# Sparse and differential attention step: the first attention takes its sample tile second and tile 7 last

## The chip, the cores and the metric

The kernel runs on one core of one Trainium2 chip. The metric is the device time of one execution in microseconds, as the median of several runs. Engines are called by the names of the profile: PE is TensorE (PEld its weight loads), DVE VectorE, ACT ScalarE, POOL GpSimd, SP SyncE, which issues the DMAs.

## The reference, cut to what matters

The program is one inference step of two layers over 1024 prompt tokens and 32 sample tokens, with model width 1024. Layer 0 has a sparse attention ("A"), layer 1 a differential one ("B"); each is followed by an output product with layer norm, and by a feed-forward part. The change lies in attention A:

```
dots = einsum('bthd,bsd->bths', qi, ki)              # indexer: 8 heads
score = einsum('bths,bth->bts', relu(dots), wi * IDX_SCALE)
_, sel = top_k(score, n_sel)                         # 256 of the prompt's keys, 40 of the sample's 160
logits = einsum('btcgd,btkcd->btcgk', q, k_sel) * 64 ** -0.5
logits = logits - slopes * abs(q_pos - sel)          # ALiBi; keys beyond the chunk limit at -inf
out = einsum('btcgk,btkcd->btcgd', softmax(logits), v_sel)
```

The prompt attends to itself in chunks of 64 tokens; the 32 sample tokens attend to 128 cached keys and their own 32. The kernel doesn't gather keys: it makes a mask for each query from the scores, adds it to the distances, and runs the attention over all keys of the tile.

## The kernel before

**Tiles and steps.** `mixer_a` cuts the queries into nine tiles: tile t of 0 to 7 has 128 queries and 128(t+1) keys, and the sample tile (number 8, `SAMPLE`) has 32 queries and 160 keys. For each tile 16 heads are worked off in 8 steps of two heads; `g` counts these steps, 0 to 71, and `heads(g)` gives tile, key group and head of a step. There are 72 steps and three more for the pipeline to drain.

**What a step does.** All engines run through the same `g`, each with its own list of work:

- PE in step g: turn the probabilities of step g-2 (`turn_over`, L634), compute the logits of step g (L619, for which the reads of step g-1 must be over), in steps 0 to 5 one or two thirds of the last projection pieces (`beside`, L588), multiply the turned probabilities of step g-2 with the values (`multiply`, L653), and on even steps turn the outputs of two finished steps (L662).
- DVE in step g: on even steps scale outputs (L998, L1000); copy every second group of turned probabilities of step g-2 out of PSUM (L991; L987 and L988 for the sample); read both heads' logits of step g (L977), adding the mask and taking the extreme of each row. Behind that come two mask operations (`islice(later, 2)`).
- ACT in step g: the other half of the copies (L754; L750 and L751 for the sample), the exponentials (L741), and the outputs' copy (L763).

**Masks.** Tiles 0 and 1 need no selection, their masks are set up in front. For tiles 2 to 7 a bit search in front of the loop finds each query's threshold. Then `masking(t)` turns scores into the mask in place, on DVE: subtraction of the threshold (L922), count (L926), tie mark (L930) and a small one (L931), scan over the ties (L936), three products (L940, L945, L950), in seven yields. `settle()` (L895 to L911, four yields, two of them counts at L902) adjusts the thresholds of tiles 6 and 7. `mask_sample()` finds the sample's 40 keys by five rounds of maximum and replace (L960, L962) and makes the mask (L966, L969), six yields. They all share `tie`, `rank` and small columns, and wait for each other through `s_mask`.

**Order around the change.** The tiles run in the order 0 to 7, then the sample. In tile t, DVE makes the mask of tile t+2: two yields behind each step's reads until that generator is empty, what is left of it at the start of the next tile at the latest. So masking is in the first four steps of tiles 0 to 5 and the sample's in the first three of tile 6; settling comes right behind tile 4's mask, in tile 2.

**Around the loop.** POOL has split the projection weights into high and low parts (L122, L124); its last pair of these, for the output product, starts when the last projection piece is done. After step 74 all of PE, ACT and DVE pass a barrier (`phase_over`). Behind it `out_norm` splits outputs and far weights (L1699, L1744, L1710, L1762, and POOL at L1617 and L1620), and PE multiplies (L1685).

Of the kernel before, what the change touches and what calls it, by code (L numbers as in the profile page):

```python
# [21 lines left out]
QT = SEQ // P  # L22
SAMPLE = QT
# [362 lines left out]
def mixer_a(c):  # L386
# [59 lines left out]
    ON_ACT = (6, 7)  # L446
    ON_DVE = (2, 3, 4, 5)
    NA, ND = len(ON_ACT), len(ON_DVE)
    ranked = list(range(2, QT))
    slope = lambda c2, m, h: 2.0 ** (-(4 * (2 * c2 + m) + h + 1) / 2)  # L450
    STEPS = 9 * 8

    def score(t):
# [6 lines left out]
    def height(t):  # L460
        return P if t < QT else NEW
# [21 lines left out]

    def heads(g):

        t, p = divmod(g, 8)
        c2, j, i = p // 4, p // 2 % 2, p % 2
        return t, c2, j, i

    def groups(t):  # L490
        b = first_blocks(t)
        return [b[j:j + 4] for j in range(0, len(b), 4)]

    def turns(g):

        gs = groups(g // 8)
        return [(m, j) for m in (0, 1) for j in range(len(gs))]

    turns_before, act_before, dve_before = [0], [0], [0]
    for g in range(STEPS):  # L500
        n = len(turns(g))
# [60 lines left out]
    def tensor(pe):  # L562
# [60 lines left out]
                        mm.then_inc(s_logit, 1)  # L623

        def turn_over(g, k):
            t, n = g // 8, height(g // 8)
            m, j = turns(g)[k]
            seq = turns_before[g] + k
            pe.wait_ge(s_exp, 2 * g + m + 1)
            if seq >= 2:  # L630
                pe.wait_ge(s_pv, seq - 1)
            for x, blk in enumerate(groups(t)[j]):
                key, size = P * (4 * j + x), NEW if blk == VNEW else P
                mm = nc.tensor.transpose(bank(c, 4 + k % 2)[0:size, P * x:P * x + n], prob[0:n, g % 3, m, key:key + size],  # L634
                                         c.ident[0:n, 0:n])
            mm.then_inc(s_tr, 1)
# [18 lines left out]
            mm.then_inc(s_pv, 1)  # L655

        def turn_outputs(grp):
            t = grp // 4
            n = height(t)
            pe.wait_ge(s_norm, grp + 1)  # L660
            for m in (0, 1):
                mm = nc.tensor.transpose(bank(c, 6 + grp % 2)[:, P * m:P * m + n],  # L662
                                         o_nat[0:n, grp % 2, m].rearrange("p i d -> p (i d)"), c.ident[0:n, 0:n])
            mm.then_inc(s_ot, 1)
# [9 lines left out]
        pe.wait_ge(s_ones, 1)  # L674
        for g in range(STEPS + 3):
            n = len(turns(g - 2)) if 2 <= g < STEPS + 2 else 0
            for k in range(min(2, n)):
# [14 lines left out]
    def scalar(act):  # L692
# [42 lines left out]
                rows(*ROWS_AFTER[sub])  # L735

        def exps(g, m):
            t = g // 8
            L, n, sl = keys_of(t), height(t), g % 3
            act.wait_ge(s_read, 2 * g + m + 1)  # L740
            nc.scalar.activation(prob[0:n, sl, m, 0:L], prob[0:n, sl, m, 0:L], ACT.Exp,  # L741
                                 bias=lowest[0:n, 2 * sl + m:2 * sl + m + 1], scale=-1.0).then_inc(s_exp, 1)

        def copy_turned(g, k):
            t = g // 8
            m, j = turns(g)[k]
            act.wait_ge(s_tr, turns_before[g] + k + 1)
            b = bank(c, 4 + k % 2).rearrange("p (x q) -> p x q", x=4)
            if t == SAMPLE:
                nc.scalar.activation(pt[:, k, 0, 0:NEW], b[:, 0, 0:NEW], ACT.Copy)  # L750
                nc.scalar.activation(pt[0:NEW, k, 1, 0:NEW], b[0:NEW, 1, 0:NEW], ACT.Copy).then_inc(s_cpa, 1)  # L751
            else:
                e = len(groups(t)[j])
                nc.scalar.activation(pt[:, k, 0:e, :], b[:, 0:e], ACT.Copy).then_inc(s_cpa, 1)  # L754

        def take_output(grp):
            t = grp // 4
            c2, j = grp // 2 % 2, grp % 2
            n = height(t)
            act.wait_ge(s_ot, grp + 1)  # L760
            src = bank(c, 6 + grp % 2, 2 * P).rearrange("p (m q) -> p m q", m=2)[:, :, 0:n]
            dst = c.o_col[:, 4 * c2:4 * c2 + 4, P * t:P * t + n].rearrange("p (m j) q -> p m j q", j=2)[:, :, j]
            nc.scalar.activation(dst, src, ACT.Copy).then_inc(s_oe, 1)  # L763

        for x, (t, ch, part) in enumerate(cells):
            n, size = height(t), cell_keys(x)[0]
# [15 lines left out]
        for b in range(31):  # L782
# [6 lines left out]
            for sub in in_pass(b):  # L789
                after(sub)  # L790
        for g in range(STEPS + 3):
            n = len(turns(g - 2)) if 2 <= g < STEPS + 2 else 0
# [13 lines left out]
    def vector(v):  # L806
# [7 lines left out]
        for x, (t, ch, part) in enumerate(cells):  # L814
            n, L, size = height(t), keys_of(t), cell_keys(x)[0]
# [34 lines left out]
        for t in ranked:  # L850
            L, j = keys_of(t), slice(t - 2, t - 1)
# [127 lines left out]
                                           lowest[0:n, 2 * sl + m:2 * sl + m + 1]).then_inc(s_read, 1)  # L979

        def copy_turned(g, k):
            t = g // 8
            m, j = turns(g)[k]
            v.wait_ge(s_tr, turns_before[g] + k + 1)
            b = bank(c, 4 + k % 2).rearrange("p (x q) -> p x q", x=4)
            if t == SAMPLE:
                nc.vector.tensor_copy(pt[:, k, 0, 0:NEW], b[:, 0, 0:NEW])  # L987
                nc.vector.tensor_copy(pt[0:NEW, k, 1, 0:NEW], b[0:NEW, 1, 0:NEW]).then_inc(s_cpv, 1)  # L988
            else:
                e = len(groups(t)[j])  # L990
                nc.vector.tensor_copy(pt[:, k, 0:e, :], b[:, 0:e]).then_inc(s_cpv, 1)  # L991

        def scale_outputs(grp):
            n = height(grp // 4)
            v.wait_ge(s_pv, turns_before[2 * grp + 2])
            o = bank(c, 6 + grp % 2, 260)[0:n].rearrange("p (x d) -> p x d", x=4)
            inv = inverse[0:n, 4 * (grp % 2):4 * (grp % 2) + 4].rearrange("p (x a) -> p x a", a=1)
            nc.vector.reciprocal(inv, o[:, :, 64:65]).then_inc(s_inv, 1)  # L998
            v.wait_ge(s_inv, grp + 1)
            nc.vector.tensor_tensor(o_nat[0:n, grp % 2].rearrange("p m i d -> p (m i) d"), o[:, :, 0:64],  # L1000
                                    inv.to_broadcast([n, 4, 64]), ALU.mult).then_inc(s_norm, 1)

        later = ()
        for g in range(STEPS + 3):
            if g % 8 == 0 and g < STEPS:
                t = g // 8
                for _ in later:
                    pass
                if t + 2 <= SAMPLE:
                    later = itertools.chain(masking(t + 2) if t + 2 < QT else mask_sample(), settle() if t == 2 else ())  # L1010
                if t >= 2:
                    v.wait_ge(s_mask, masks)
            n = len(turns(g - 2)) if 2 <= g < STEPS + 2 else 0
            if g >= 4 and g % 2 == 0:
                scale_outputs((g - 4) // 2)
            if n:
                copy_turned(g - 2, 1)
            if g < STEPS:
                read_logits(g, 0)
            if n > 2:  # L1020
                copy_turned(g - 2, 3)
            if g < STEPS:
                read_logits(g, 1)
                for _ in itertools.islice(later, 2):
                    pass
# [1536 lines left out]
```

## Time and profile before

| what | value |
|---|---|
| median of 3 runs | 3197.73 us (3195.79 to 3198.46) |
| profiled execution | 3199.4 us, of which its span is 3197.5 us |
| mean granted clock of TensorE | 0.982 |
| TensorE busy | 3074.4 us, 96% |
| VectorE busy | 1513.2 us, 47% |
| ScalarE busy | 884.6 us, 28% |
| GpSimd busy | 1015.5 us, 32% |
| attention A's loop, first reads to barrier | 281.7 to 623.7 us |

The profiled execution is one run; its span reaches from its first to its last instruction, and 1.9 us of its time lie around the span. It stands 1.7 us above the median. The loop that the change touches is 342 of these 3197 us. A granted clock of 1.00 is 2.4 GHz for TensorE and 0.50 is 1.2 GHz; a value between them is a stretch with some of both. Matmuls overlap, so a group of them shows a busy time from the first start to the last modelled end.

### The profile page before, as it was taken

How to read it: one execution, taken by the hardware profiler on the slowest of the kernel's cores; microseconds unless marked ns; L12 is line 12 of the kernel's file. 1: busy time of each engine (PE TensorE's matmuls, PEld its weight loads, DVE VectorE, ACT ScalarE, POOL GpSimd, SP SyncE). 2: the span in 40 equal slices, each digit the busy share in tenths (PEclk: the TensorE clock that was granted, in tenths of full speed). 3: DMA queues.
4: the chain of work that ended last, by engine and by line, in shares of the span. 5: the costliest groups of instructions: out<-in, count | busy, mean ns of one | idle time of the engine just before them, and what ended most of it. 6: DMA issues, size and time to landing. Idle time of an engine off the chain costs nothing.

```text
span 3197.5 us, 49157 instructions
## 1 busy us (share of the span) xinstructions
PE 3074.4 (96%) x19621; PEld 2880.4 (90%) x19621; DVE 1513.2 (47%) x2914; ACT 884.6 (28%) x1915; POOL 1015.5 (32%) x495
## 2 busy tenths in 40 slices
PE   8799999899999999999989999989999999999996
PEld 8498777688999999999988999977899999999996
DVE  1898855543533343333454555565345333343335
ACT  2476544342111101111134544453300111100112
POOL 2132000135543333433242222214444433333422
PEclk9899999899999999999999999999999999999998
DMA  2122000112311111111012111111222111111101
GB/s 87 28 61 53 1 1 1 41 40 73 95 53 46 46 46 39 52 46 46 14 57 63 43 49 50 37 41 66 70 85 60 52 46 46 46 46 39 52 0 55
DMA packets 209372, 149.75 MB, mean 47 GB/s; under 512 B 28914, under 2 KB 195764, under 8 KB 209236
## 3 DMA queue, kind: packets, MB, share of 16 engines
q1 hardware_dynamic: 209236, 147.85, 15.5%
q8 instruction: 96, 1.57, 0.2%
q14 instruction: 40, 0.33, 0.0%
HBM read 128.09 MB, written 19.73 MB: 46 GB/s over the span
## 4 chain that ended last, share of the span: by engine, by line
PE 88%; DVE 6%; ACT 2%; issue 2%; POOL 1%; DMA 1%; SPq 0%; POOLq 0%; ACTq 0%; DVEq 0%
PE psum L153 49%; PE psum L2081 16%; PE psum L1685 6%; PE psum L653 4%; DVE junk L867 2%; PE psum L634 2%; PE psum L619 2%; PE psum L1273 2%; PE psum L1247 2%; PE psum L1261 1%; PE psum L588 1%; PE psum L572 1%; DVE bias L826 1%; PE psum L1222 0%; PE psum L1639 0%
## 5 line engine op out<-in xcount | busy, mean ns | idle before, releaser
L153 PE MATMUL psum<-x_hi,w_hi 128*128 128x352 f32 (+1 forms) x3192 | 1040.9, 326 | 10.0 <-POOL x_lo L1628 4.1
L153 PE MATMUL psum<-x_hi,w_lo 128*128 128x352 f32 (+1 forms) x3192 | 1027.7, 322 | 0.0
L153 PE MATMUL psum<-x_lo,w_hi 128*128 128x352 f32 (+1 forms) x3192 | 1027.6, 322 | 0.0
L122 POOL TENSOR_TENSOR w_hi<-w_raw,zeros 128x1024 fp32r<-128x1024 f32 (+1 forms) x209 | 381.5, 1825 | 1522.6 <-PE psum L153 939.2
L153 PEld LDWEIGHTS psum<-x_hi,w_hi 128*128 128x128 f32 (+1 forms) x3192 | 601.6, 188 | 12.1 <-issue 11.3
L153 PEld LDWEIGHTS psum<-x_lo,w_hi 128*128 128x128 f32 (+1 forms) x3192 | 602.4, 189 | 0.5
L153 PEld LDWEIGHTS psum<-x_hi,w_lo 128*128 128x128 f32 (+1 forms) x3192 | 601.0, 188 | 0.4
L124 POOL TENSOR_TENSOR w_lo<-w_raw,w_hi 128x1024 fp32r<-128x1024 f32 (+1 forms) x209 | 485.8, 2324 | 16.4
L2342 DVE TENSOR_TENSOR gate<-psum,gate 128x352 f32<-128x352 f32 x120 | 63.0, 525 | 725.3 <-PE psum L153 725.3
L2081 PE MATMUL psum<-h_hi,w_hi 128*128 128x352 f32 x1056 | 341.2, 323 | 1.2 <-DVE h_lo L2364 1.0
L2081 PE MATMUL psum<-h_lo,w_hi 128*128 128x352 f32 x1056 | 338.6, 321 | 0.0
L2081 PE MATMUL psum<-h_hi,w_lo 128*128 128x352 f32 x1056 | 338.4, 320 | 0.0
L2307 DVE TENSOR_TENSOR o_col<-psum,o_col 128x352 f32<-128x352 f32 x528 | 263.3, 520 | 157.4 <-PE psum L2081 155.2
L2081 PEld LDWEIGHTS psum<-h_hi,w_hi 128*128 128x128 f32 x1056 | 198.3, 188 | 1.9 <-issue 1.6
L2081 PEld LDWEIGHTS psum<-h_lo,w_hi 128*128 128x128 f32 x1056 | 198.6, 188 | 0.0
L2081 PEld LDWEIGHTS psum<-h_hi,w_lo 128*128 128x128 f32 x1056 | 198.1, 188 | 0.0
L2346 DVE TENSOR_TENSOR h_lo<-gate,h_hi 128x352 fp32r<-128x352 f32 x120 | 198.0, 1675 | 0.0
L653 PEld LDWEIGHTS psum<-valsA,ptA 128*128 128x128 f32 (+1 forms) x1216 | 145.1, 188 | 38.3 <-issue 17.5
L2236 ACT ACTIVATE h_hi<-gate 128x352 fp32r<-128x352 f32 x120 | 59.8, 498 | 426.9 <-DVE gate L2342 426.9
L653 PE MATMUL psum<-valsA,ptA 128*128 128x65 f32 (+1 forms) x1216 | 162.7, 277 | 3.9 <-DVE ptA L991 3.0
L2233 ACT ACT_TABLE_LOAD x20 | 25.7, 1283 | 478.8 <-PE psum L153 460.0
L1458 DVE CUSTOM_DVE_ANT_0 probB<-psum,distB 128x128 f32<-128x128 f32 (+5 forms) x144 | 96.4, 707 | 123.3 <-PE psum L1247 122.4
(461 smaller groups left out, 4085.3 us busy)
## 6 DMA issues: line engine op xcount, KB each, us to landing
w_raw<-in_ffn_w_dram SPq DMA_DIRECT2D x132, 512.0 KB
w_raw<-in_b_w_in_dram SPq DMA_DIRECT2D x24, 512.0 KB
w_raw<-in_ple_w_gate_dram SPq DMA_DIRECT2D x16, 512.0 KB
x_nat<-in_x_prompt_dram SPq DMA_DIRECT2D x8, 512.0 KB, 8.2
w_raw<-in_a_w_in_dram SPq DMA_DIRECT2D x8, 512.0 KB
w_raw<-in_a_w_in_dram SPq DMA_DIRECT2D x16, 256.0 KB
x_rows<-x_rows SPq DMA_DIRECT2D x8, 512.0 KB, 2.6
out_new_b_v_prompt_dram<-valsB SPq DMA_DIRECT2D x8, 512.0 KB, 3.3
```

The source lines that it names most:

```text
L122: nc.gpsimd.tensor_tensor(c.w_hi[s][:, 0:kc], c.w_raw[s][:, 0:kc], zero, ALU.add).then_inc(c.split[s], 1)
L124: nc.gpsimd.tensor_tensor(c.w_lo[s][:, 0:kc], c.w_raw[s][:, 0:kc], c.w_hi[s][:, 0:kc].bitcast(F32), ALU.subtract).then_inc(c.split[s], 1)
L153: last = c.nc.tensor.matmul(out, w, x, start=(n == 0), stop=(n == 3 * len(terms) - 1))
L619: mm = nc.tensor.matmul(c.psum[0:n, 1024 * m + a:1024 * m + a + size], queries[rows, 4 * c2 + 2 * i + j, q:q + n], keys[rows, c2, key:key ...
L634: mm = nc.tensor.transpose(bank(c, 4 + k % 2)[0:size, P * x:P * x + n], prob[0:n, g % 3, m, key:key + size], c.ident[0:n, 0:n])
L653: mm = nc.tensor.matmul(c.psum[0:n, at:at + 65], pt[0:size, k, x, 0:n], vals[0:size, blk, 2 * c2 + m, :], start=(j == 0 and x == 0), stop= ...
L867: nc.vector.tensor_scalar(junk[t][:, :], score(t), level[:, t - 2:t - 1], 0.0, ALU.is_ge, ALU.add, accum_out=count[:, t - 2:t - 1]).then_i ...
L1458: nc.vector.tensor_tensor_reduce(prob[:, sl, m, 0:L], c.psum[:, 1024 * m:1024 * m + L], dist[:, o:o + L], slope(h), -LOWEST, ALU.add, ALU.min,
L1685: mm = nc.tensor.matmul(out, o[t % 2][:, u, 0:n], ww[:, cols], start=(j == 0 and x == 0), stop=(j == KC - 1 and x == 2))
L2081: mm = nc.tensor.matmul(o, w[s][:, m, :], h[:, j, piece(t)], start=(j == 0 and k == 0), stop=(j == 1 and k == 2))
L2307: nc.vector.tensor_tensor(o, src, o, ALU.add).then_inc(s_da, 1)
L2346: nc.vector.tensor_tensor(h_lo[:, j, piece(done)], gate[:, 1, piece(done)], h_hi[:, j, piece(done)].bitcast(F32), ALU.subtract).then_inc(s ...
```

## The change

The tiles run in the order 0, sample, 1, 2, ... 7. All functions that derived the tile from `g` or from the group of outputs now look it up in `TILES`. The masks are made in that same order by one generator, `all_masks()`: sample, 2, 3, 4, 5, settling, 6, 7. It runs on without regard to tile boundaries, two yields a step, until it is empty; at the start of a tile only what that tile still lacks is made first. What each mask computes is unchanged.

```
+    TILES = (0, SAMPLE, 1, 2, 3, 4, 5, 6, 7)
...
     def heads(g):
-        t, p = divmod(g, 8)
-        c2, j, i = p // 4, p // 2 % 2, p % 2
-        return t, c2, j, i
+        p = g % 8
+        return TILES[g // 8], p // 4, p // 2 % 2, p % 2
...
     def turns(g):
-        gs = groups(g // 8)
+        gs = groups(TILES[g // 8])
...
-            t, n = g // 8, height(g // 8)
+            t = TILES[g // 8]
+            n = height(t)
...
-            t = grp // 4
+            t = TILES[grp // 4]
...
-        later = ()
+        made = {0, 1}
+
+        def all_masks():
+            settled = False
+            for t in TILES:
+                if t < 2:
+                    continue
+                if t in ON_ACT and not settled:
+                    settled = True
+                    yield from settle()
+                yield from mask_sample() if t == SAMPLE else masking(t)
+                made.add(t)
+
+        later = all_masks()
         for g in range(STEPS + 3):
             if g % 8 == 0 and g < STEPS:
-                t = g // 8
-                for _ in later:
-                    pass
-                if t + 2 <= SAMPLE:
-                    later = itertools.chain(masking(t + 2) if t + 2 < QT else mask_sample(), settle() if t == 2 else ())
+                t = TILES[g // 8]
+                while t not in made:
+                    next(later, None)
                 if t >= 2:
                     v.wait_ge(s_mask, masks)
```

The lines that change a tile's lookup in `exps`, `copy_turned` (ACT and DVE), `take_output` and `scale_outputs` are of the same kind and are left out here.

## Rows read from the trace of the kernel before

**Rows 1.** The page: one engine line of busy times, and the chain by engine.
```profile
PE 3074.4 (96%) x19621; PEld 2880.4 (90%) x19621; DVE 1513.2 (47%) x2914; ACT 884.6 (28%) x1915; POOL 1015.5 (32%) x495
...
PE 88%; DVE 6%; ACT 2%; issue 2%; POOL 1%; DMA 1%; SPq 0%; POOLq 0%; ACTq 0%; DVEq 0%
```

**Rows 2.** Windows: tile 1, tile 3, sample's first part and rest.
```profile
core 0: us, PE busy (x) PEld busy (x) DVE busy (x) ACT busy (x) POOL busy (x), PEclk, DMA share, GB/s
...
303.25:322.34 19.09, 17.84 (x127) 12.84 (x128) 15.54 (x57) 11.07 (x28) 0.00 (x0) 1.00 0.09 29
...
347.98:379.41 31.43, 30.99 (x226) 23.61 (x226) 24.07 (x57) 16.81 (x28) 0.00 (x0) 1.00 0.01 1
...
604.55:610.40 5.85, 5.85 (x71) 4.15 (x72) 3.55 (x22) 3.40 (x14) 0.00 (x0) 1.00 0.01 3
610.40:623.80 13.40, 11.83 (x87) 7.32 (x86) 4.67 (x28) 4.40 (x21) 0.13 (x1) 0.51 0.00 0
```

**Rows 3.** Waits, 278 to 660 us: total, times, longest.
```profile
PE psum L1685 <- POOL far_lo4A L1620: 3.4, 1, 3.4
...
PE psum L653 <- DVE ptA L991: 3.0, 5, 1.0
```

**Rows 4.** Timeline of DVE, 298 to 330 us: start, duration, instruction.
```profile
299.15 0.18 DVE L998 RECIPROCAL inverseA<-psum 128x4 f32<-128x4 f32 x1 [1.32 <-PE psum L653]
...
307.68 0.16 DVE L998 RECIPROCAL inverseA<-psum 128x4 f32<-128x4 f32 x1
...
308.21 0.41 DVE L991 COPY ptA<-psum 128x256 f32<-128x256 f32 x1
...
309.23 0.75 DVE L940 SCALAR_TENSOR_TENSOR tieA<-rankA,countA,tieA 128x512 bf16<-128x512 int16 x1
...
327.97 0.16 DVE L998 RECIPROCAL inverseA<-psum 128x4 f32<-128x4 f32 x1
```

**Rows 5.** Timeline of DVE in one even step of the sample tile.
```profile
608.34 0.17 DVE L998 RECIPROCAL inverseA<-psum 32x4 f32<-32x4 f32 x1 [0.31 <-PE psum L653]
...
608.89 0.17 DVE L987 COPY ptA<-psum 128x32 f32<-128x32 f32 x1
...
609.17 0.31 DVE L977 CUSTOM_DVE_ANT_0 probA<-psum,bias 32x160 f32<-32x160 f32 x1
...
609.67 0.07 DVE L977 DVE_READ_ACCUMULATOR2_ANT lowestA<- 32x1 f32 x1
```

**Rows 6.** Windows of tieA's instructions, tiles 3 to 7's masks; two groups by line.
```profile
303.25:322.34 19.09, 4.47 (x7) 1.00 0.09 29
322.34:347.98 25.64, 7.77 (x11) 1.00 0.00 1
347.98:379.41 31.43, 6.20 (x7) 1.00 0.01 1
379.41:426.00 46.59, 7.07 (x7) 1.00 0.01 1
426.00:471.00 45.00, 7.93 (x7) 1.00 0.00 1
...
L922 DVE TENSOR_SCALAR bias<-bias,levelA,signA 128x384 f32<-128x384 f32 (+5 forms) x6 | 5.5, 909 | 0.0
...
L931 DVE TENSOR_SCALAR countA<-countA 128x1 f32<-128x1 f32 x6 | 0.9, 147 | 0.0
```

**Rows 7.** Timeline of POOL and DVE around the two last weight splits.
```profile
281.57 2.41 POOL L124 TENSOR_TENSOR w_lo<-w_raw,w_hi 128x1024 fp32r<-128x1024 f32 x1
...
282.13 2.07 DVE L922 TENSOR_SCALAR bias<-bias,levelA,signA 128x384 f32<-128x384 f32 x1
...
300.84 2.36 POOL L124 TENSOR_TENSOR w_lo<-w_raw,w_hi 128x1024 fp32r<-128x1024 f32 x1
```

**Rows 8.** Timeline: tile 7's last scaling on DVE; POOL's first instruction behind the barrier.
```profile
604.66 0.18 DVE L998 RECIPROCAL inverseA<-psum 128x4 f32<-128x4 f32 x1 [0.97 <-PE psum L653]
...
623.67 1.89 POOL L1617 TENSOR_TENSOR far_hi0A<-w_raw,zeros 128x1024 fp32r<-128x1024 f32 x1 [320.48 <-ACTq L2513]
```

**Rows 9.** Window in the indexer's scores, where the clock fell and came back.
```profile
144.70:148.50 3.80, 3.33 (x12) 2.50 (x12) 3.56 (x6) 1.80 (x3) 1.50 (x1) 0.71 0.00 0
```

More of the change, by code:

```diff
@@ L744, in copy_turned @@
         def copy_turned(g, k):
-            t = g // 8
+            t = TILES[g // 8]
             m, j = turns(g)[k]
@@ L756, in take_output @@
         def take_output(grp):
-            t = grp // 4
+            t = TILES[grp // 4]
             c2, j = grp // 2 % 2, grp % 2
@@ L981, in copy_turned @@
         def copy_turned(g, k):
-            t = g // 8
+            t = TILES[g // 8]
             m, j = turns(g)[k]
@@ L993, in scale_outputs @@
         def scale_outputs(grp):
-            n = height(grp // 4)
+            n = height(TILES[grp // 4])
             v.wait_ge(s_pv, turns_before[2 * grp + 2])
@@ L1001, in scale_outputs @@
                                     inv.to_broadcast([n, 4, 64]), ALU.mult).then_inc(s_norm, 1)
-        later = ()
+        made = {0, 1}
[10 more added lines that the diff above has]
+        later = all_masks()
         for g in range(STEPS + 3):
             if g % 8 == 0 and g < STEPS:
-                t = g // 8
-                for _ in later:
-                    pass
-                if t + 2 <= SAMPLE:
-                    later = itertools.chain(masking(t + 2) if t + 2 < QT else mask_sample(), settle() if t == 2 else ())
+                t = TILES[g // 8]
+                while t not in made:
+                    next(later, None)
                 if t >= 2:
```

## The prediction

> **What bounds the kernel now.** The page comes first: TensorE is busy 96% of the span and carries 88% of the chain that ended last; VectorE carries 6% [rows 1]. So a change counts only where TensorE waits, or where its clock is low. I then cut the attention loop into stages. From tile 1 to tile 7 TensorE is nearly always busy at clock 1.00: tile 1 takes 19.1 us (17.84 busy, so 2.23 us of TensorE work a step), tile 3 31.4 us (30.99 busy, 3.9 a step). The two exceptions are the end and the beginning. The sample tile, last, starts with TensorE full at 1.00 for 5.85 us, some 1.8 us a step, and then goes on for 13.4 us at 0.51 [rows 2]. And while masks are made in steps 9, 10, 18, 21 and 26, TensorE waits five times for VectorE's half of the turned probabilities, 3.0 us in all [rows 3].
>
> In those steps VectorE is the bound. Its order in a step is fixed: scaling of outputs (even steps), copy of turned probabilities, two logit reads, two mask operations. The even step of tile 1 that starts at 307.68 has its copy at 308.21 and its reads over at 309.23, with no idle time: 1.55 us without masks, and 1.02 in an odd step, which has no scaling. The masks then follow in the same queue, 309.23 on [rows 4]. The sample tile takes 0.55 for the scaling, 0.28 for the copies, 0.50 for the reads: 1.33 and 0.78 us [rows 5].
>
> **The change, part by part.** Nothing is added or removed: the same matrix products, masks and copies run in another order, no DMA is issued elsewhere, and SP's and POOL's queues stay as they are. A mask is seven yields, the sample's mask six (five rounds of max and replace, then one), settling four; two yields are taken a step. Before, each tile began one mask and the rest of its steps had none, so the masks of tiles 5, 6, 7 lay in tiles 3, 4, 5, where a step has 3.9 us of TensorE work or more. After, the generator runs straight on: sample in steps 0 to 2, tile 2 in 3 to 6, tile 3 in 6 to 9, tile 4 in 10 to 13, tile 5 in 13 to 16, settling in 17 and 18, tile 6 in 19 to 22, tile 7 in 22 to 25. The 52 yields are used up at step 25. Steps 0 to 5 carry projection, and 1.4 us of mask work per step hides under it. Step 6 has none, so from there to 25 VectorE's sum counts: the end of tile 0, all of the sample tile, all of tile 1, two steps of tile 2.
>
> *Mask work in steps 6 to 25.* The operations that touch the tie tile take 4.47 us for tile 3, 7.77 for tile 4 with settling's two counts, 6.20, 7.07 and 7.93 for tiles 5, 6, 7: 33.4. The subtraction, L922, is 5.5 for six tiles, of which tile 2's took 2.07 [rows 6, 7]: 3.4 for five. Small ones (five of L931 at 0.15, settling's five two-column ones, about the same each) and tile 2's last (0.55) add 2.1. That is 38.9 us of durations; successive starts lie about 0.04 us closer than durations say, over some 35 operations, which leaves 37.3.
>
> *VectorE's own part.* Ten steps at the sample's rate, 5 x (1.33 + 0.78) = 10.6, ten at tile 1's, 5 x (1.55 + 1.02) = 12.9: 23.5 [rows 4, 5]. The total is 60.8 us for twenty steps, 3.0 each, against TensorE's 1.8 to 2.23. Single steps run from 1.8 to 5.4 us (step 24: 1.8 of its own and tile 7's scan and tie product), and in each the VectorE sum is above TensorE's work at full clock. Before, step 6 begins on VectorE at 299.15 and the step that corresponds to the new 26, the third of tile 2, at 327.97 [rows 4]: 28.8 us. The front grows by 60.8 - 28.8 = **+32.0 us**, and now contains the sample tile.
>
> *What goes at the end.* Tile 7's last product ends where VectorE's reciprocal starts, 604.66, and the barrier is passed when POOL starts on the output weights, 623.67 [rows 8]: 19.0 us. After, tile 7 still needs its own scaling, turn and copy, about 1.8 us (0.6 VectorE, 0.45 TensorE, 0.4 ScalarE and the gaps): **-17.3**. The sample's logits leave tile 7's last two steps, 0.4 us of TensorE each, but the exponentials and copies they covered then show; I take half, **-0.4** (0 to -0.8). The last three waits for masks (steps 18, 21 and 26, 1.7 of the 3.0 us) partly go, since steps 26 on have no masks, while the wait just behind the last mask stays: **-0.8**. The two in tile 1 are inside the 28.8 already.
>
> *POOL.* The first L922 took 2.07 us where its size asks for about 0.5; POOL was in L124 from 281.57, 2.41 us long, and it ended just behind that. The same pair of POOL operations runs again at the end of the projections, L124 at 300.84 for 2.36 us [rows 7]. Before, no mask lay there. After, steps 6 and 7 put tile 2's last operation and tile 3's L922 there, with nothing to cover them. Price 0 to 2.7 us; I take **+2.3**, since the row shows nearly the whole wait. The old wait of this kind, in step 0, lay under projection and gives nothing back.
>
> *The clock.* At full clock TensorE keeps up everywhere, but will it be granted? In 604.55 to 610.40 it was 1.00 with the sample's small products, from 610.40 on 0.51, although TensorE had been busy all 5.85 us [rows 2]. After, the same small products come spread over 2.8 us a step. I expect the half level (1.2 GHz) somewhere in steps 9 to 12. In the sample tile this is free: TensorE then needs some 2.5 us a step (13.4 us for the last five and what closes them), VectorE 2.8. In tile 1 it isn't: 2 x 2.23 = 4.5 against 2.5 to 4.2. Elsewhere a dip under dense work ended quickly (mean 0.71 over 3.8 us is 2.2 us at half) [rows 9]. So two or three steps of tile 1 run TensorE-bound, at 1.0 to 1.4 us more each: **+3**, with 0 below (clock never matters) and +9 above (half through step 25: eight steps of 4.2 to 5.4 us, 36.9, against VectorE's 28.8, and 1 in steps 16 and 17).
>
> The Trainium skill ("TensorE: Matmul & The Clock Gate", section "HAM oscillation") puts such falls down to gaps in which TensorE idles. By that rule a step's wait of one to two microseconds would not lower it, and the clock term would be 0. The trace disagrees at 610.4, where no gap stood ahead of the fall.
>
> **Sum.** 32.0 - 17.3 - 0.4 - 0.8 + 2.3 + 3 = +18.8 us. The profiled execution took 3199.4 us (span 3197.5, 1.9 around it), so 3218.2; it lies 1.7 above the median of the runs shown, 3197.73, and the forecast for the median is **3216 us**, 0.57% more. What lies behind the barrier I cost at nothing: there TensorE waits for POOL's far_lo4 (3.4 us, rows 3), a chain that starts with the barrier, whatever the clock before.
>
> **Rivals.** *The clock stays up, or returns at once* (17%): 3213. For it: tile 1 kept 1.00 with TensorE waiting. *The clock stays down through tile 1* (16%): 3222. For it: VectorE-bound steps leave TensorE idle a third of the time. Against: at half clock TensorE is the bound, and full. *The masks are hidden* (3%), the other side: if small steps had room for them, the sample tile would cost 8 x 1.8 = 14.4 instead of 19, tile 7's tail 1.8, and the five waits would go: 14.4 + 1.8 - 19.0 - 0.4 - 2.1 = -5.3, 3192. It decides where TensorE's step is longer than VectorE's; for it speaks only that VectorE is busy 4.67 of 13.4 us in the old sample tile, against it that two mask operations average 1.9 us. *Half hidden* (5%): within 0.2%.
>
> **How the numbers follow.** The forecast's case has 55%, 4% is for what I do not see above 3225. 0.2%, 6.4 us, is about what a measurement tells from no change. Slower by more: 55 + 17 + 16 + 4 = 92%; same 5%; faster 3%. The range goes from 3209 (no clock term, no POOL wait, sum 13.5, less 2 for an error of a tenth in each of twenty steps) to 3225 (clock down through tile 1, POOL 2.7, and the same 2 added).
>
> **What would show it.** In the profile of after: steps 6 to 25 with VectorE busy without gaps for some 61 us, TensorE waiting for the copy at L991 and L987 (some 20 us in place of 3.0); L922 of tile 3 near 300 at 2 us; tile 7's last product at full clock and the barrier 2 us behind it; a granted clock near 0.5 from the sample tile into tile 1. I am wrong if VectorE idles there, if steps 26 on are not as before, or if the output stage takes another length.

## The result, and the profile after

The changed kernel takes 3220.08 us (median of 6 runs, 3216.47 to 3222.11) against 3197.65 us (6 runs): a ratio of 1.0065, 95% interval 1.0054 to 1.0075. The forecast was 3216 us, within 3209 to 3225.

The page's line of busy times and its chain by engine, after:

```profile
PE 3090.8 (96%) x19621; PEld 2890.7 (90%) x19621; DVE 1517.3 (47%) x2914; ACT 885.8 (28%) x1915; POOL 1016.5 (32%) x495
...
PE 89%; DVE 6%; ACT 2%; issue 2%; POOL 1%; DMA 1%; SPq 0%; POOLq 0%; ACTq 0%; DVEq 0%
```

The counts are those of [rows 1]: the same instructions run. TensorE's busy time is 16.4 us longer, though its work is the same. So something beside waiting has grown, and the windows show what: the granted clock. They run from step 6 (302.06) to the fall of the clock, then to its return, to step 26 (369.25), to the last product (646.45), to the barrier (648.11):

```profile
core 0: us, PE busy (x) PEld busy (x) DVE busy (x) ACT busy (x) POOL busy (x), PEclk, DMA share, GB/s
302.06:306.90 4.84, 2.80 (x21) 2.01 (x20) 4.70 (x13) 1.97 (x7) 4.15 (x2) 0.93 0.00 0
306.90:329.00 22.10, 21.98 (x158) 14.94 (x158) 20.77 (x81) 9.35 (x35) 0.00 (x0) 0.50 0.08 26
329.00:350.70 21.70, 21.31 (x97) 14.11 (x95) 18.41 (x53) 7.67 (x22) 0.00 (x0) 0.50 0.00 1
350.70:369.25 18.55, 14.04 (x92) 9.69 (x90) 18.14 (x41) 7.38 (x17) 0.00 (x0) 0.96 0.01 1
369.25:646.45 277.20, 266.23 (x1932) 210.21 (x1931) 135.18 (x314) 129.16 (x195) 0.00 (x0) 0.99 0.00 1
646.45:648.11 1.66, 0.44 (x2) 0.20 (x2) 0.60 (x2) 0.38 (x1) 0.00 (x0) 1.00 0.00 0
```

What the reader is to see: in the first and fourth rows VectorE is full (4.70 of 4.84, 18.14 of 18.55) and TensorE is not. In the two rows between, 43.8 us long, TensorE is busy 43.3 us at clock 0.50 and VectorE has gaps: 22.10 + 21.70 - 20.77 - 18.41 = 4.6 us. The loop from step 6 to the barrier takes 648.11 - 302.06 = 346.05 us, against 623.67 - 299.15 = 324.52 before [rows 4, 8]: +21.5. Of the other 1.3 us of the span's 22.8, +2.9 lie ahead of step 6 and -1.6 behind the barrier. The 2.9 are not shown to be the change's: e4 below runs the same program up to step 7 and began step 6 at 298.49, ahead of the 299.15 of the kernel before.

The waits, 281 to 665 us:

```profile
PE psum L654 <- DVE ptA L992: 6.9, 6, 2.1
...
PE psum L1697 <- DVE o_lo0A L1756: 3.8, 1, 3.8
```

And behind the barrier, 648.11 to 705 us:

```profile
PE psum L1697 <- POOL far_lo4A L1632: 3.5, 1, 3.5
```

Against [rows 3] the waits for the turned probabilities have gone from 3.0 to 6.9 us, in six places. That is not the 20 us that I named as the sign: at half clock TensorE stretches over the time in which it would have waited. Behind the barrier the waits are those of before: 3.8 and 3.5 us for VectorE's and GpSimd's pieces, 3.6 and 3.4 before.

The timeline of GpSimd and VectorE at the first place where VectorE is late:

```profile
303.75 2.54 POOL L124 TENSOR_TENSOR w_lo<-w_raw,w_hi 128x1024 fp32r<-128x1024 f32 x1
```

```profile
302.06 0.18 DVE L999 RECIPROCAL inverseA<-psum 128x4 f32<-128x4 f32 x1 [0.20 <-PE psum L654]
...
303.39 0.69 DVE L951 SCALAR_TENSOR_TENSOR bias<-tieA,dist 128x384 f32<-128x384 bf16 x1
304.12 2.45 DVE L923 TENSOR_SCALAR bias<-bias,levelA,signA 128x512 f32<-128x512 f32 x1
306.49 0.28 DVE L992 COPY ptA<-psum 128x128 f32<-128x128 f32 x1
```

L923 of tile 3 takes 2.45 us beside GpSimd's L124, where the same operation took 0.54 before; VectorE's copy for TensorE's next products stands behind it, TensorE waits 2.04 us for that copy, and the clock falls at the end of the wait, between 306.0 and 306.9. And the end, by the timeline:

```profile
646.45 0.18 DVE L999 RECIPROCAL inverseA<-psum 128x4 f32<-128x4 f32 x1 [1.20 <-PE psum L654]
...
647.62 0.38 ACT L764 ACTIVATE o_col<-psum 128x256 f32<-128x256 f32 x1 [4.08 <-PE psum L663]
...
648.11 1.89 POOL L1629 TENSOR_TENSOR far_hi0A<-w_raw,zeros 128x1024 fp32r<-128x1024 f32 x1 [341.82 <-ACTq L2525]
```

1.66 us from the last product to the barrier, in place of 19.0 [rows 8].

### The profile page after: what moved, and what is told of

Read it like the earlier page. It is cut to its first block, busy times and chain, and to the rows that moved or that the text cites. A ratio compares the mean times of both kernels' runs of the same rounds, so it can differ in the third digit from the quotient of the medians.

```text
span 3220.3 us, 49157 instructions
## 1 busy us (share of the span) xinstructions
PE 3090.8 (96%) x19621; PEld 2890.7 (90%) x19621; DVE 1517.3 (47%) x2914; ACT 885.8 (28%) x1915; POOL 1016.5 (32%) x495
## 4 chain that ended last, share of the span: by engine, by line
PE 89%; DVE 6%; ACT 2%; issue 2%; POOL 1%; DMA 1%; SPq 0%; POOLq 0%; ACTq 0%; DVEq 0%
PE psum L153 49%; PE psum L2093 16%; PE psum L1697 6%; PE psum L654 4%; PE psum L619 2%; PE psum L635 2%; DVE junk L868 2%; PE psum L1285 2%; PE psum L1259 2%; PE psum L1273 1%; PE psum L588 1%; PE psum L572 1%; DVE bias L827 1%; PE psum L1234 0%; PE psum L1651 0%
## 5 line engine op out<-in xcount | busy, mean ns | idle before, releaser
L124 POOL TENSOR_TENSOR w_lo<-w_raw,w_hi 128x1024 fp32r<-128x1024 f32 (+1 forms) x209 | 486.5, 2328 | 16.4
L654 PE MATMUL psum<-valsA,ptA 128*128 128x65 f32 (+1 forms) x1216 | 169.6, 283 | 8.4 <-DVE ptA L992 6.9
L2245 ACT ACT_TABLE_LOAD x20 | 25.7, 1283 | 478.8 <-PE psum L153 460.0
```

The lines of the kernel that those rows point to most:

```text
L124: nc.gpsimd.tensor_tensor(c.w_lo[s][:, 0:kc], c.w_raw[s][:, 0:kc], c.w_hi[s][:, 0:kc].bitcast(F32), ALU.subtract).then_inc(c.split[s], 1)
L654: mm = nc.tensor.matmul(c.psum[0:n, at:at + 65], pt[0:size, k, x, 0:n], vals[0:size, blk, 2 * c2 + m, :], start=(j == 0 and x == 0), stop= ...
```

## The experiments

How the numbers are read. "Loop" is the time from the reciprocal of step 6 to GpSimd's first instruction behind the barrier, in the one profiled execution; a tile's time is from the reciprocal of its first step to that of the next tile's. The kernel before was run beside each (median 3197.65 us beside the changed kernel, 3199.2 to 3199.5 beside the experiments). "Over before" is the median less that.

| kernel | median, us | ratio, 95% | over before | loop over 324.5 | tile behind 0 | next | next |
|---|---|---|---|---|---|---|---|
| before | | | | 0 | t1 18.8 | t2 25.3 | t3 31.5 |
| after | 3220.1 | 1.0065 (1.0054 to 1.0075) | 22.4 | 21.5 | sample 22.7 | t1 29.2 | t2 28.7 |
| e1 order alone | 3215.6 | 1.0052 (1.0039 to 1.0066) | 16.4 | 14.4 | sample 18.2 | t1 31.4 | t2 26.5 |
| e2 masks alone | 3221.1 | 1.0066 (1.0052 to 1.0080) | 21.8 | 21.6 | t1 30.4 | t2 32.7 | t3 31.6 |
| e3 one yield | 3206.8 | 1.0024 (1.0015 to 1.0033) | 7.5 | 6.3 | sample 17.3 | t1 28.0 | t2 23.4 |
| e4 after, clock held | 3213.8 | 1.0045 (1.0032 to 1.0059) | 14.6 | 15.0 | sample 21.5 | t1 25.7 | t2 26.8 |
| e5 e1, two products | 3213.5 | 1.0044 (1.0030 to 1.0057) | 14.0 | 14.5 | sample 22.5 | t1 28.3 | t2 25.3 |
| e6 GpSimd's split late | 3221.5 | 1.0066 (1.0053 to 1.0080) | 22.0 | 22.7 | sample 22.7 | t1 30.8 | t2 30.3 |
| e7 sample before tile 7 | 3202.0 | 1.0006 (0.9997 to 1.0015) | 2.6 | 5.0 | t1 18.8 | t2 25.3 | t3 31.5 |
| e8 old order, one yield | 3199.4 | 0.9998 (0.9989 to 1.0007) | 0.0 | 5.2 | t1 17.3 | t2 23.6 | t3 30.8 |
| e9 e1, one dense block | 3208.3 | 1.0017 (1.0005 to 1.0029) | 8.8 | 5.2 | sample 18.3 | t1 23.2 | t2 25.3 |
| e10 e1, three products | 3204.7 | 1.0011 (1.0003 to 1.0020) | 5.3 | 5.6 | sample 20.2 | t1 19.6 | t2 26.7 |
| e11 e2, clock held | 3213.5 | 1.0038 (1.0024 to 1.0052) | 14.0 | 14.2 | t1 25.5 | t2 31.1 | t3 30.7 |
| e12 e3, three products | 3200.1 | 1.0002 (0.9993 to 1.0010) | 0.9 | 2.3 | sample 20.2 | t1 20.8 | t2 23.4 |

The two columns of differences agree within 3 us but for e8, whose profiled execution lay 4.8 us above its median, and e9, whose lay 3.0 below. That of e1 lay 7.0 us below its median, that of e4 5.2 below, that of e2 6.0 above and that of the changed kernel 2.0 above. So a single loop difference is good to some microseconds, and so are the differences between two of them.

**e1, the order alone.** The new order, but each mask begun where the old pacing had it, two tiles ahead:

```
-        later = all_masks()
+        def one(t):
+            yield from mask_sample() if t == SAMPLE else masking(t)
+            made.add(t)
+            if t == 4:
+                yield from settle()
+
+        later = ()
+        BEGUN = {0: SAMPLE, 1: 2, 2: 3, 3: 4, 4: 5, 5: 6, 6: 7}
...
-                while t not in made:
-                    next(later, None)
+                for _ in later:
+                    pass
+                later = one(BEGUN[g // 8]) if g // 8 in BEGUN else ()
```

> The new order of the tiles, but each mask is begun at a tile's start and the rest of that tile has none, as before: the sample's in tile 0, tile 2's in the sample tile, tile 3's in tile 1, and so on. Theory (the masks run on into small tiles are the cost): 3200 us, 3197 to 3205. The sample tile in its new place then takes about 16.5 us and a few more for the clock, and 17.3 go at the end. Rival (a small tile early is the cost in itself, by the clock that falls in it and stays down): 3212 or more.

Measured 3215.6 us, +14.4 us in the loop, nearly all of it at the low clock. Windows of this kernel:

```profile
306.00:308.00 2.00, 2.00 (x24) 1.37 (x24) 1.97 (x11) 1.33 (x6) 0.00 (x0) 1.00 0.00 0
308.00:310.00 2.00, 2.00 (x20) 1.35 (x20) 1.81 (x10) 1.09 (x5) 0.00 (x0) 0.72 0.01 4
310.00:312.00 2.00, 2.00 (x20) 1.42 (x18) 0.35 (x4) 1.04 (x5) 0.00 (x0) 0.50 0.03 8
...
311.00:353.00 42.00, 42.00 (x210) 28.62 (x210) 20.45 (x83) 15.26 (x46) 0.00 (x0) 0.50 0.00 1
```

While the clock is low VectorE is busy 20.45 of 42.00 us, so it bounds nothing there; TensorE is full without a gap, at half clock. Ahead of the fall, at 308.9, TensorE had been full for 3.0 us, in the sample's steps. But before that it had waited for VectorE, since tile 2's mask is made in the first steps of the sample tile here:

```profile
305.93 0.53 PE L654 MATMUL psum<-valsA,ptA 128*32 128x65 f32 x4 [0.83 <-DVE ptA L989]
```

So what started this fall is not separated by this run: the sample's products or that wait. The falls with no wait of TensorE in the 5 us ahead are those of the kernel before at 610.4 [rows 2] and of e5, e7 and e8 below. Tile 1 costs 31.4 us in place of 18.8, +12.5 of the loop's 14.4. In the kernel before, the same products of tile 1 kept clock 1.00 [rows 2]. So the order alone costs two thirds of the change's price, and VectorE's sum is no part of it.

**e2, the masks alone.** The old order with the generator that runs straight on:

```
-    TILES = (0, SAMPLE, 1, 2, 3, 4, 5, 6, 7)
+    TILES = (0, 1, 2, 3, 4, 5, 6, 7, SAMPLE)
```

> The old order of the tiles, but the masks made one behind the other, two yields a step, until all are made. Theory: VectorE's sum for steps 6 to 22 is about 56.5 us where they took 44.7, and POOL's split adds 2 and the clock up to 3: 3211 to 3215 us. Rival (it takes both, the sample tile early and the masks): 3198 to 3201.

3221.1 us: the masks alone cost as much as the whole change. Its windows from step 6:

```profile
304.93:311.00 6.07, 4.12 (x20) 2.64 (x20) 5.93 (x21) 2.21 (x7) 2.28 (x1) 0.69 0.27 89
311.00:335.00 24.00, 24.00 (x100) 17.71 (x99) 20.40 (x60) 9.17 (x22) 0.00 (x0) 0.50 0.00 1
335.00:341.00 6.00, 6.00 (x34) 4.16 (x33) 4.16 (x14) 2.45 (x6) 0.00 (x0) 0.75 0.00 0
341.00:382.14 41.14, 35.45 (x218) 26.35 (x218) 37.21 (x95) 17.41 (x35) 0.00 (x0) 0.88 0.00 1
```

No step of the sample tile is near, and the clock falls all the same, behind steps in which VectorE makes TensorE wait (4.12 of 6.07 busy). TensorE waits 1.76 and 1.07 us for VectorE's copies in that first row. So the clock falls in two situations: among the sample's small products without a wait, and among other small steps behind waits for VectorE. Whether the two have one cause isn't shown. The two costs, 14.4 and 21.6, do not add to 21.5 in the changed kernel: where the masks set the pace, half clock is mostly hidden, and where the clock sets it, the masks are. The 21.6 leave something out: in this order GpSimd's split meets an earlier mask operation (L941 of tile 3 takes 2.31 us, for the 0.75 of [rows 4]), mostly ahead of step 6. From step 4 to the barrier it is +23.6.

**e3, one yield a step.** The changed kernel with its masks at half the pace:

```
-                for _ in itertools.islice(later, 2):
+                for _ in itertools.islice(later, 1):
```

> The changed kernel with one yield a step in place of two; all masks are then made by step 51 and each is ready in time. Theory: a step's VectorE sum is then near TensorE's work, little waits, and the time is 3200 us, 3196 to 3204. Rival (the order alone costs): 3210 or more.

3206.8 us. The pace of the masks is worth 13.3 us of the median. The clock was 0.50 in 317 to 341 here too, and tile 1 took 28.0 us, 9.1 more than before; tile 2 took 1.9 less than before. The remaining loss lies in tile 1, at the low clock.

**e4, the clock held in the changed kernel.** Three matrix products that serve nothing are added to each of steps 7 to 25, into banks that are free then:

```
+            if 7 <= g < 26:
+                for b in (1, 3, 1):
+                    nc.tensor.matmul(bank(c, b), c.x_hi[:, 0, 0:P], c.x_hi[:, 0, 0:512], start=True, stop=True)
             for k in range(n):
                 multiply(g - 2, k)
```

> The changed kernel with three more matrix products of 128 by 512 in each of steps 7 to 25, which write banks 1 and 3 that nobody reads there. At full clock they add 0.64 us to TensorE's 1.8 to 2.2 a step, still below VectorE's sum in nearly all steps. Theory (the low clock costs some 5 us of the 22): if the clock is held, 3214 to 3217 us, with VectorE without gaps. Rival (the clock costs nothing, VectorE is the bound anyway): 3220 or more. If the clock isn't held, the products cost more than they bring, and the run tells nothing of the price.

3213.8 us. Windows from step 6 to step 26, and the next 17 us:

```profile
298.49:361.02 62.53, 57.92 (x421) 40.48 (x420) 61.25 (x183) 26.05 (x81) 4.17 (x2) 1.00 0.03 10
361.02:378.00 16.98, 15.82 (x118) 12.21 (x118) 10.94 (x36) 9.15 (x19) 0.00 (x0) 1.00 0.00 1
```

The clock is 1.00 throughout and VectorE is busy 61.25 of 62.53 us, where I had worked out 60.8 and 2.3 behind GpSimd, 63.1. The loop is 6.6 us shorter than the changed kernel's, 4.7 of it ahead of step 26 and 1.9 behind. That, and not 3, is what the clock costs in the changed kernel, and more as far as the added products cost e4 time. The medians lie 6.3 us apart, and 7.8 when each is set against its own runs of the kernel before. The clock was up in all five executions of e4 (mean 0.983 to 0.987, the changed kernel's six 0.976 to 0.979), and it stayed up although TensorE waited for VectorE's copies five times, up to 1.43 us.

By stage the 6.6 us are: nothing in steps 6 and 7, 1.1 in the sample tile, 3.5 in tile 1 (29.2 against 25.7), nothing in steps 24 and 25, 1.9 behind step 26.

**e5, two products in the order alone.** e1 with two such products (banks 1 and 3) in each of steps 8 to 16.

> The new order with masks paced as in the run with that pacing, and two more matrix products of 128 by 512 in each of steps 8 to 16, which write banks that nobody reads there. They add 0.43 us a step, 3.9 in all, where TensorE is the bound. Theory (in the new order with paced masks the low clock, from the sample tile through all of tile 1, is nearly the whole cost): the clock stays at 1.00, tile 1 takes about 19 us in place of 31.4, and the time falls from 3215.6 to some 3203. Rival (the order costs in another way, the clock only goes along with it): 3214 or more, tile 1 at 25 us or more.

3213.5 us. The clock was not held: it fell near 313 and was 0.50 from 317 to 347. TensorE had no wait ahead of the fall in this run. The sample tile became 4.3 us longer, with the added products in it, and tile 1 still took 28.3. So this run says nothing of a held clock, and e10 repeats it with three, begun one step earlier.

**e6, GpSimd's second split of output weights later,** behind a wait for the outputs of step 32, so that none lies beside L923 (L924 here):

```
+    c.late_split = s_norm
...
+            if A and u == 1:
+                g.wait_ge(c.late_split, 16)
             split_unit(c, g, name, 0, u, KC)
```

> The changed kernel, with POOL's split of the second output weight unit held back until the outputs of step 32 are scaled, so that it lies behind all masks. Theory (POOL's split holds VectorE in step 6): the subtraction of tile 3's mask takes 0.54 us in place of 2.45 and steps 6 and 7 together 2 us less; the clock also falls later, so 3215 to 3218 us in place of 3220.1. Rival (what is won there is lost again at TensorE's low clock or behind): 3220.

The edit did its part. Timelines of VectorE and GpSimd, then a window of this kernel:

```profile
304.62 0.55 DVE L924 TENSOR_SCALAR bias<-bias,levelA,signA 128x512 f32<-128x512 f32 x1
```

```profile
400.02 2.36 POOL L124 TENSOR_TENSOR w_lo<-w_raw,w_hi 128x1024 fp32r<-128x1024 f32 x1
```

```profile
368.00:374.00 6.00, 6.00 (x25) 4.59 (x25) 4.26 (x9) 1.65 (x4) 0.00 (x0) 0.50 0.01 3
...
374.00:376.00 2.00, 2.00 (x11) 1.67 (x13) 0.04 (x1) 1.07 (x3) 0.00 (x0) 0.53 0.00 0
```

L924 takes 0.55 us and steps 6 and 7 take 4.25 us instead of 6.29: the 2.0 us of the GpSimd term are shown. The Trainium skill ("GPSIMD Engine Reference", section "Key points") says that GpSimd shares its SBUF interfaces with VectorE and contends with some of its instructions; the trace agrees, 2.45 us beside L124 and 0.55 without. Yet the time stays, 3221.5 us: the clock fell at about 307.6, in a wait of 0.77 us, and stayed at 0.50 until 375.5, some 68 us in one stretch. In the changed kernel it was 43.8 us and, behind a second fall, 7 more; tiles 1 and 2 took 1.6 us more each here. A wait of 2 us taken away was worth nothing, because the clock took it back.

**e7, the sample tile before tile 7,** masks paced as in e1: `TILES = (0, 1, 2, 3, 4, 5, 6, SAMPLE, 7)`.

> Order 0 to 6, sample, 7, masks as in the kernel before. Tile 7 still ends the loop at full density, so the drain is short as in the changed kernel, but the sample tile lies in front of dense steps. The sample costs 14.4 to 19 us there in place of 17.3, and the clock must come back in tile 7. If dense steps bring it back at once: 3196 to 3201. If it stays low as it does in tile 1 of the new order: up to 64 us at half, 3210 or more.

3202.0 us, the same as before within what can be told. Tiles 1 to 6 take what they took. From the start of the eighth tile (526.9) to the barrier it is 101.6 us, against 96.6 (from 527.1). Windows about the sample's steps:

```profile
540.90:546.00 5.10, 5.10 (x63) 3.60 (x60) 3.10 (x21) 3.24 (x14) 0.00 (x0) 0.94 0.02 5
546.00:570.00 24.00, 22.66 (x124) 12.70 (x124) 10.25 (x33) 9.31 (x22) 0.00 (x0) 0.66 0.00 1
```

The clock falls just ahead of 546, in the sample's steps again; TensorE's timeline shows no wait from 526 on, and no mask was being made, so neither a gap nor VectorE is needed for this fall. Under tile 7 it comes back at about 555, falls once more from 559 to 565 behind a wait of 1.04 us, and then stays up. So the end that was saved (19.0 to 1.7 us) is not a gain by itself: the sample tile costs as much or more wherever it is put, since it takes the clock down and the tile behind it pays. That rests on two new places, the second and the eighth.

**e8, the old order, one yield a step,** with two added products in steps 65 to 73 to hold the clock at the end.

> The old order, masks made one behind the other with one yield a step, and the two more matrix products in steps 65 to 73. The waits for masks in tiles 1 to 3 go (up to 3.0 us), and the clock is held through the sample tile at the end: 4 to 5 us less there, of which the products take back up to 3. 3192 to 3197 us. Rival (nothing to win: one yield a step still makes waits and the clock isn't held): 3199.

3199.4 us, no difference. The windows of the sample tile:

```profile
609.00:612.00 3.00, 3.00 (x32) 2.00 (x32) 1.37 (x9) 1.22 (x7) 0.00 (x0) 1.00 0.03 5
612.00:615.00 3.00, 3.00 (x19) 1.56 (x17) 0.82 (x6) 0.91 (x5) 0.00 (x0) 0.51 0.00 0
```

In this execution the products did not hold the clock, which fell at 612, and the sample's eight steps took 5.9 us more (32.35 against 26.43). It is not the typical one: its time, 3204.2 us, is the highest of the eleven and its mean clock, 0.981, the lowest; the other ten have 0.983 to 0.985, against 0.981 to 0.983 in the runs of the kernel before beside them. So this trace doesn't show what the products did in the others. One yield a step made tiles 1 to 3 shorter by 1.6, 1.7 and 0.7 us and the steps ahead of them longer by 1.5. What it gives without the products, some 2.6 us by these rows, is below what can be told, and was not run.

**e9, a dense block.** e1 with twelve such products in step 16, the first of tile 1, and none elsewhere.

> New order with the masks begun two tiles ahead, as in the run with the order alone, and one block of twelve 128x512 matmuls in step 16, the first step of tile 1. Before it the sample tile still lowers the granted clock. Theory 1 (the sample's small products lower the clock, and it comes back only behind dense work): the block costs 3 to 5 us, the clock is 1.00 behind it, tile 1 takes 18.8 us plus the block, 23 instead of 31.4; the loop takes 331 us instead of 338.9, the median is about 3207. Theory 2 (tile 1's own products keep the clock down, whatever stands before them): the clock is 0.50 again within some microseconds, tile 1 takes 31 plus the block, 35; the loop 343, the median 3219.

3208.3 us. Windows around the block:

```profile
323.00:325.00 2.00, 2.00 (x9) 1.19 (x8) 1.11 (x7) 0.58 (x3) 0.00 (x0) 0.50 0.00 0
325.00:327.00 2.00, 2.00 (x7) 1.60 (x6) 1.51 (x7) 0.51 (x1) 0.00 (x0) 0.65 0.00 0
327.00:329.00 2.00, 2.00 (x13) 1.19 (x12) 0.00 (x0) 0.00 (x0) 0.00 (x0) 1.00 0.00 0
329.00:331.00 2.00, 2.00 (x20) 1.24 (x20) 0.88 (x5) 0.90 (x5) 0.00 (x0) 1.00 0.00 0
```

The clock comes back within the block and stays at 1.00 through all of tile 1, with tile 1's own products and nothing added. The block costs 4.3 us (9.86 for tile 1's first two steps, 5.55 in the kernel before) and tile 1 is 8.2 us shorter than in e1, the block included. So tile 1's products keep a full clock but did not bring it back in e1.

**e10, three products in the order alone.** e1 with `(1, 3, 1)` in each of steps 7 to 17.

> New order with the masks begun two tiles ahead, and three added 128x512 matmuls in each of steps 7 to 17, where the earlier run had two in steps 8 to 16 and lost the clock at 313. Theory 1 (density of the steps ahead of tile 1 decides): the clock stays at 1.00 to the end of tile 1; the sample tile takes 1.8 us a step and 0.64 more for the added products, 19.5 us, tile 1 18.8 and 1.3; the loop 328 us, the median 3205. Theory 2 (the sample's products lower it whatever stands beside them, unless VectorE spaces them as it does when masks are made there): the clock falls in the sample tile again, which then takes 25 us, tile 1 28 to 31, the median 3213 to 3220.

3204.7 us. Windows of the sample tile with the two steps ahead of it, of tile 1, and of a stretch in tile 2:

```profile
302.62:326.49 23.87, 23.87 (x207) 16.77 (x206) 14.51 (x76) 11.16 (x42) 3.97 (x2) 1.00 0.08 24
326.49:346.12 19.63, 19.63 (x144) 13.75 (x145) 15.53 (x60) 10.86 (x30) 0.00 (x0) 1.00 0.00 1
...
353.00:355.00 2.00, 1.06 (x10) 0.93 (x9) 1.97 (x7) 0.30 (x1) 0.00 (x0) 0.98 0.00 0
355.00:357.00 2.00, 2.00 (x12) 1.67 (x11) 1.81 (x5) 1.39 (x4) 0.00 (x0) 0.50 0.00 0
```

The clock holds, and tile 1 takes 19.6 us, 0.8 above before. In tile 2 a mask makes TensorE wait (1.06 busy of 2.00) and the clock dips just behind it, for some 3 us, at a cost of 1.4 us for the tile. The wait alone did not decide it: it was 0.94 us, and the same wait in the same step was 0.93 in the kernel before, in e5 and in e9, where the clock stayed at 1.00.

**e11, the masks alone, clock held.** e2 with three products in each of steps 7 to 25.

> Old order with the masks made straight on, two yields a step, as in the run with the masks alone (3221, 77.2 us from step 6 to step 26), and three added 128x512 matmuls in each of steps 7 to 25 to hold the clock. Theory 1 (VectorE's sum is the bound there, the half clock adds to it): the clock is 1.00; VectorE has 37.3 us of masks, 12.9 for ten steps at tile 1's rate, some 14.5 for the ten of tiles 2 and 3, and 2.1 behind POOL, 67 us from step 6 to step 26, against 55.8 in the kernel before; the loop takes 336 us instead of 346.1, the median is about 3211. Theory 2 (the masks alone cost through VectorE, the clock is not the matter): 77 us and 3221 again.

3213.5 us. Two windows of it:

```profile
305.00:311.00 6.00, 6.00 (x22) 4.35 (x22) 5.79 (x20) 1.48 (x4) 0.00 (x0) 0.50 0.30 90
...
317.00:323.00 6.00, 6.00 (x43) 4.59 (x42) 5.89 (x19) 2.90 (x9) 0.00 (x0) 1.00 0.00 1
```

The clock was 0.50 for one stretch of 6.6 us, from 304.6 behind a wait of 1.76 us to 311.2, then 1.00 to the end of the masks. In e2, with the same wait and no added products, it stayed at 0.50 until 338. Step 6 to step 26 took 69.2 us against 77.2 without the products and 67 worked out; that stretch is part of the difference. Some 1.6 of the 2.1 us behind POOL in the 67 lie ahead of step 6 (L944 of tile 3 takes 2.31 us there), so the miss is nearer 4 us than 2, and from step 4 to the barrier the loop is +16.2. With the clock up, VectorE's sum (busy 66.8 of the 69.2 us) is most of what the masks cost, here too: +13.3 us over before's 55.8 to step 26, of the loop's 14.2.

**e12, both remedies.** e3 with three products in each of steps 7 to 17.

> Both remedies at once, to see whether the new order can be brought below the kernel before: new order, one yield a step in place of two, and three added 128x512 matmuls in each of steps 7 to 17. Theory 1 (VectorE's load and the granted clock are the whole cost, and they are separate terms): clock 1.00 from step 6 to tile 2, the sample tile 20.2 us as in the run with three products, tile 1 19.6 instead of 28.0, tile 2 23.4, tile 3 30.4, the rest as with one yield: a loop of 325.6 us against 324.5 before, the median about 3201, the same as before within what can be told. Theory 2 (something else of the new order costs as well): the loop stays above 329, the median above 3204. A loop under 322 us, with a median under 3197, would make it a version that beats both kernels; by the sum the added products eat what the order gives.

3200.1 us, the same as before. The loop took 326.8 us, 1.2 more than the sum of the parts; the windows of the sample tile with two steps, and of tile 1:

```profile
303.06:326.97 23.91, 23.91 (x207) 16.78 (x206) 15.74 (x81) 11.17 (x42) 3.99 (x2) 1.00 0.08 24
326.97:347.74 20.77, 20.77 (x150) 14.26 (x150) 17.25 (x61) 11.64 (x32) 0.00 (x0) 1.00 0.00 1
```

TensorE is full at 1.00 and does not wait. With the pace of the masks and the clock mended, the new order loses nothing; by an estimate (11 steps of 0.64 to 0.80 us, as in e4) the added products take 7 to 9 us, so they eat what the order could give. No version that beats the kernel before was found.

## Why the prediction was right, point by point

**VectorE's sum, +32.0: right.** Held at full clock (e4) the twenty steps take 62.5 us for 60.8 and 2.3 worked out. TensorE idles 4.6 of them there; with the added products taken off it would be 17 to 20, for the 20 that I named. (An estimate: 19 steps of 0.64 us by the expectation, or of the 0.80 us that e4's timeline shows from the first of the three to the product behind them.) Two slips in the working, 37.3 for 37.5 and -17.3 for -17.2, make 0.3 us together and change nothing. In the changed kernel itself the stretch takes 67.2 us: the front grew by 38.4, for 37.3 with the terms for GpSimd and the clock. The operations on the tie tile took 33.95 us in steps 6 to 25 of the changed kernel, for 33.4 read from [rows 6].

**The end, -17.3: right in its own terms,** 1.66 us for 1.8. What e7 adds is that this is no independent gain, since the sample tile takes the clock down in its new place too.

**GpSimd, +2.3: right in size** (2.04 us by e6), and worth nothing by itself.

**Cover of the sample's logits and the waits for masks, -0.4 and -0.8.** From step 26 to the last product it took 277.2 us against 276.7 before [rows 4, 8], +0.5 where -1.2 was forecast. In e4, at full clock, it took 636.30 - 361.02 = 275.3, -1.4. So the two terms together were right at full clock (they are not told apart), and the difference goes with a second fall of the clock in tile 2, behind a wait of 2.06 us. Windows of the changed kernel:

```profile
366.00:368.00 2.00, 1.96 (x14) 1.37 (x14) 2.00 (x5) 1.51 (x3) 0.00 (x0) 0.92 0.00 0
368.00:374.00 6.00, 5.66 (x24) 4.62 (x24) 3.54 (x10) 2.02 (x5) 0.00 (x0) 0.50 0.01 3
```

**The clock, +3: the right mechanism, mis-sized.** The step that failed is the one that put the half level "somewhere in steps 9 to 12" and let it return after two or three steps of tile 1. It fell at 306.9 at the latest, in step 7, behind a wait at the L923 that I had priced myself, and stayed for 43.8 us, six steps into tile 1. By the comparison with e4 it costs 6.6 us. In tile 1, where I had put the 3, it is 3.5. The rest of the miss are two places that I had put at nothing: the sample tile, "free" in the prediction, 1.1, and the second fall in tile 2, 1.9. With 6.6 the sum is 32.0 - 17.3 - 0.4 - 0.8 + 2.3 + 6.6 = 22.4, against 21.5 in the loop and 22.4 between the medians. That the last two figures are equal is chance: single executions of one kernel differ by more. What lies behind the barrier, put at nothing, was -1.6.

**The order of the causes was not in the prediction.** I read the cost as VectorE's, with the clock as a small term on top. e1 and e2 show two causes that each suffice for most of it: 14.4 us by the order alone, almost all of it clock, and 21.6 by the masks alone. With the clock up they are small and large, 5.6 (e10) and 14.2 (e11), beside 15.0 for both (e4), the added products included in all three. In e10 these take an estimated 7 to 9 us (11 steps of 0.64 to 0.80), so nothing would be left there of the order's cost. They overlap since VectorE and TensorE are bound in the same steps.

**The rivals.** "The clock stays down through tile 1" (3222) came nearest in the clock, which stayed down for six of tile 1's eight steps, and in the number. Not in its price: it wanted 9 us of tile 1, which cost 3.5. VectorE needed 25.7 us there at full clock (e4), and the half level counted only in the four steps 18 to 21. "The clock stays up" is excluded by every run in the new order without added products (after, e1, e3, e6). "The masks are hidden" is excluded by e4: at full clock VectorE still sets the pace.

**The rule that I weighed,** from the Trainium skill ("TensorE: Matmul & The Clock Gate", section "HAM oscillation"), puts falls of the clock down to gaps in which TensorE idles. I had read it as leaving the clock alone in waits of one to two microseconds, with a clock term of 0. The trace disagrees twice. The clock fell behind such waits (2.04 us in the changed kernel, 1.76 in e2, 0.77 in e6), and it cost 6.6 us. And it fell without any wait: in the kernel before at 610.4, in e5 at 313, in e7 at 546 and in e8 at 612, TensorE had been full for at least 5 us. Nor does the length of a wait decide: behind 1.62 us in e2 (at 349.5) and 1.43 in e4 the clock stayed up. What decided, the rows of 32 or the shortness of the products or something else, these runs do not separate.

## What to carry to other kernels

Before moving a stage of small products forward, look at the granted clock in the rows of that stage: a stage that lowers the clock at the end of a loop pays only for itself there, and the stage behind it pays too when it stands in front. When work is moved on an engine that is not the bound, sum that engine step by step against the others' shortest steps, not against the average share (47% here). And a wait that is removed is only worth its length if the clock does not take it back: read the clock of an experiment before its time.

## What was not expected of the hardware

- The half level lasted far longer than TensorE's busy time would suggest: 42 us with TensorE busy 42.00 us in e1, and some 68 us in e6. Tile 1's products are among them, which keep 1.00 in the kernel before and in e9. It came back near 350.7 (after), 353 (e1), 338 (e2), 342 (e3), 347 (e5) and 375 (e6), at different steps. Added 128x512 products brought it back sooner: the block of twelve in e9, which runs from 324.43 to 328.35, with the clock back at about 326, and the three a step of e11, within 6.6 us. What ended the others is open.
- With two added products of that size in a step the clock fell in the sample tile (e5, and the profiled execution of e8); with three it did not (e4, e10, e12). The three also began one step earlier than e5's two, so the number alone is not shown to decide.
- The same wait of TensorE in the same step, 0.93 and 0.94 us, left the clock at 1.00 in the kernel before, e5 and e9 and was followed by a fall in e10.
- Two of VectorE's mask instructions took three to four and a half times as long beside GpSimd's L124: L923 2.45 us for 0.55 (after, e6), L941 2.31 for 0.75 (e2, before).
